# An HGRN2 stage inside a projection loop: small column-tiled products in two groups per unit instead of six, and a common PSUM bank for three levels

## The reference

```python
def hybrid_layer(x, ...):
    z = rmsnorm(x, norm_g) @ w_in          # 1024 -> 4608 columns
    ...
    q = jax.nn.silu(qc) * (C_KDIM ** -0.5)
    g = lbh + (1.0 - lbh) * jax.nn.sigmoid(fc)
    v = ic
    oc, s_fin = hgrn2(q, 1.0 - g, v, jnp.log(g), s0)

def hgrn2(q, k, v, logf, s0):              # scan over chunks
    def step(state, inp):
        bcum = jnp.cumsum(ft, axis=2)
        o_inter = einsum('bhld,bhdv->bhlv', qt * exp(bcum), state)
        diff = bcum[:, :, :, None, :] - bcum[:, :, None, :, :]
        decay = exp(where(causal, diff, -inf))
        attn = einsum('bhtd,bhtsd,bhsd->bhts', qt, decay, kt)
        o = o_inter + einsum('bhts,bhsv->bhtv', attn, vt)
        new_state = exp(blast) * state + einsum('bhsd,bhsv->bhdv', kt * exp(blast - bcum), vt)
        return new_state, o
```

## Time and profile before

| | us |
|---|---|
| median of 3 runs (lowest, highest) | 1688.76 (1685.87, 1689.35) |
| span of the profiled execution | 1690.4 |
| TensorE matmuls busy in it | 1588.9 (94%) |
| VectorE, ScalarE, GpSimd busy | 976.2 (58%), 823.9 (49%), 628.9 (37%) |
| HGRN stage, from the first to the last unit's steps | about 458 to 1075 |
| barrier between `front` and `attend_project` | about 1077 to 1080.7 |

### The profile page before, as it was taken

One profiled execution on the slowest core, in us unless ns is written; L12 is line 12 of the kernel. 1 busy time (PEld: TensorE's weight loads), 2 busy tenths in 40 slices (PEclk: granted clock), 3 DMA queues, 4 the chain that ended last, 5 costly groups with the idle time before them and its releaser, 6 DMA issues. The chain is left out here.

```text
span 1690.4 us, 38531 instructions
## 1 busy us (share of the span) xinstructions
PE 1588.9 (94%) x15345; PEld 1345.8 (80%) x15345; DVE 976.2 (58%) x2066; ACT 823.9 (49%) x1603; POOL 628.9 (37%) x754
## 2 busy tenths in 40 slices
PE   6999998899999999999999998899999888999997
PEld 5988887889988888878888787886777667777775
DVE  3436763433377777677676776325666556555652
ACT  4426876212256555566767776244777631111110
POOL 1102221200076666666666665203645602121110
PEclk9999998999999999999999999897999989999999
DMA  6310111124412212121110211447993284775651
GB/s 212 114 51 29 34 39 59 50 73 135 141 38 62 57 36 79 41 75 30 56 46 26 67 31 43 118 112 178 239 237 85 78 258 127 247 229 189 208 171 47
DMA packets 196287, 175.27 MB, mean 104 GB/s; under 512 B 84915, under 2 KB 180686, under 8 KB 193806
## 3 DMA queue, kind: packets, MB, share of 16 engines
q1 hardware_dynamic: 196110, 172.82, 35.6%
HBM read 123.18 MB, written 52.84 MB: 104 GB/s over the span
## 5 line engine op out<-in xcount | busy, mean ns | idle before, releaser
L49 PE MATMUL f_bank<-c_ht,c_whi 128*128 128x384 f32 (+1 forms) x864 | 321.0, 372 | 5.7 <-DVE c_wlo L893 5.7
L51 PE MATMUL f_bank<-c_ht,c_wlo 128*128 128x384 f32 (+1 forms) x864 | 303.3, 351 | 0.0
L50 PE MATMUL f_bank<-c_ht,c_whi 128*128 128x384 f32 (+1 forms) x864 | 302.9, 351 | 0.0
L842 ACT ACTIVATE f_scr<-f_scr 128x384 f32<-128x384 f32 (+1 forms) x210 | 114.0, 544 | 206.3 <-POOL f_scr L617 206.2
L1056 DVE TENSOR_TENSOR f_scr<-f_scr 128x192 f32<-128x192 f32 (+1 forms) x210 | 105.4, 502 | 137.4 <-ACT f_scr L842 137.1
L49 PEld LDWEIGHTS f_bank<-c_ht,c_whi 128*128 128x128 f32 x864 | 162.7, 188 | 21.4 <-DVE c_wlo L893 6.5
L50 PEld LDWEIGHTS f_bank<-c_ht,c_whi 128*128 128x128 f32 x864 | 163.2, 189 | 9.7 <-issue 1.1
L51 PEld LDWEIGHTS f_bank<-c_ht,c_wlo 128*128 128x128 f32 x864 | 163.0, 189 | 9.4
L616 POOL TENSOR_TENSOR f_scr<-f_scr 128x192 f32<-128x192 f32 (+1 forms) x210 | 134.6, 641 | 40.7 <-PE f_tps L1240 37.8
L1047 DVE COPY_PREDICATED f_scr<-f_scr,f_tps 128x384 f32<-128x384 int32 (+1 forms) x210 | 130.6, 622 | 18.1 <-PE f_tps L1240 9.5
L49 PE MATMUL a_s<-a_whi,a_mhi 128*128 128x512 f32 (+1 forms) x306 | 125.8, 411 | 4.5 <-DVE a_y L2471 4.5
(11 more groups left out here) (401 smaller groups left out, 3816.2 us busy)
## 6 DMA issues: line engine op xcount, KB each, us to landing
f_wraw<-in_w_in SPq DMA_DIRECT2D x27, 512.0 KB, 4.0
zs<-f_stage SPq DMA_DIRECT2D x48, 192.0 KB, 2.4
a_k<-in_ck SPq DMA_DIRECT2D x48, 192.0 KB, 5.7
a_v<-in_cv SPq DMA_DIRECT2D x48, 192.0 KB
f_scr<-in_xp SPq DMA_DIRECT2D x16, 512.0 KB, 4.2
a_x<-in_xp SPq DMA_DIRECT2D x16, 512.0 KB, 5.6
out_y_prompt<-a_y SPq DMA_DIRECT2D x16, 512.0 KB, 2.9
zt<-f_stage SPq DMA_DIRECT2D x38, 192.0 KB, 1.8
```

The lines of the kernel that those rows point to most:

```text
L49: nc.tensor.matmul(out, w_hi, m_hi, start=start, stop=False)
L50: nc.tensor.matmul(out, w_hi, m_lo, start=False, stop=False)
L51: return nc.tensor.matmul(out, w_lo, m_hi, start=False, stop=stop)
L842: A(lev[i % 3][:, :n], lev[i % 3][:, :n], ACT.Exp).then_inc(S["expd"], 1)
```

## The change

`HPLAN` is written anew, and with it:
- TensorE's small products of a unit stand in two groups. In slot 3: `hk`, `ho` of the unit before, and `hpa`: the diagonal, level 1, and one product for levels 64, 32 and 16 together. In slot 0: `hu` and `hpb` (levels 8, 4, 2). VectorE takes them in two rows of three, `hta` and `htb`; the states are `hv`.
- Pair products have three PSUM banks (`tps[0:3]`, the third shared with the transposes `kp`). Levels 64, 32 and 16 are written into one bank and taken with one mask, `far_mask`, the sum of their three; so a unit has six takes instead of eight. `level_blocks` cuts all blocks to 32 keys; `outputs` works in blocks of 32 instead of 64.
- Level 1 no longer goes through `hm`: its decay is the forget gate of one position, 1 - key. `h1`: ScalarE writes 1 - key into `gone` (Identity), VectorE multiplies the query in (`stepped_query`), and the product takes the key itself as its other side.
- `hgrn_gates` ends with the second table load; the two Ln are a step of their own, `hl`, in slot 4. The key's Ln takes the unscaled key with the scale inside; GpSimd scales the key in `hc1`, slot 0. `sqo` (the squared output) lies in PSUM.
- `hgrn_gates` of a unit now waits for the second pair product of the unit before (`2 * BURST * (v - 1) + 2`). `query` waits also for `qd_ready` and for all `xlev` of the unit before. `hk`'s transposes wait for the takes of the unit before; the merged product waits for `kd_copied`. `load_v` is issued at `hpa`.

```diff
-HPLAN = {0: [("hp6", 2), ("hm0", 1), ("hm1", 1)],
-         1: [("ho", 2), ("hpd", 1), ("hp0", 1), ("hd", 1), ("hm2", 1)],
-         2: [("hf", 2), ("hm3", 1), ("hp1", 1), ("hx", 1), ("hp2", 1), ("hm4", 1), ("he", 1), ("hw", 2), ("hk", 1)],
-         3: [("hu", 1), ("hm5", 1), ("hp3", 1), ("hg", 2), ("hs", 0)],
-         4: [("hm6", 1), ("hp4", 1), ("hn", 0)],
-         5: [("hp5", 1), ("hq", 0), ("hy", 0)]}
+NM = NL - 1
+BURST = 3
+HPLAN = {0: [("hu", 2), ("hpb", 2), ("htb", 2), ("hv", 2), ("hm0", 1), ("hc1", 1)],
+         1: [("hm1", 1), ("h1", 1)],
+         2: [("hm2", 1), ("hd", 1), ("hx", 1)],
+         3: [("hk", 1), ("ho", 2), ("hpa", 1), ("hta", 1), ("hf", 2), ("hs", 0), ("hm3", 1), ("hw", 2)],
+         4: [("hm4", 1), ("hm5", 1), ("hl", 0), ("he", 1), ("hn", 0)],
+         5: [("hq", 0), ("hy", 0), ("hg", 2)]}
...
-    return [(c, c + hs, hs) for c in range(0, P, 2 * hs)]
+    return [(c + x, c + hs, hs) for x in range(0, hs, QUAD) for c in range(0, P, 2 * hs)]
...
-        lp, kp, up = tps[0:2], tps[2], tps[3]
-        gnorm = op[:, 0:AW]
+        lp, kp, up = tps[0:3], tps[2], tps[3]
+        gnorm, sqo = op[:, 0:AW], op[:, FW // 2:FW]
...
-    pairs_of_level = lambda i: (NL + 1) * (i // NL) + i % NL + 2
+    pairs_of_level = lambda i: 2 * BURST * (i // NM) + max(i % NM + 1, BURST)
...
-                elif kind == "hs":
+                elif kind == "hc1":
                     h, g, t0, n, nt, _ = unit(a)
-                    pool.wait_ge(S["f_out"], BASE + a + 1)
+                    pool.wait_ge(S["log_k"], BASE + a + 1)
                     G.tensor_scalar(key[:, :n], key[:, :n], lbl[:, 1, h:h + 1], None, ALU.mult).then_inc(S["gated"], 1)
...
-                    act.wait_ge(S["pairs"], BASE + (NL + 1) * (v - 1) + 1)
+                    act.wait_ge(S["pairs"], BASE + 2 * BURST * (v - 1) + 2)
                     act.wait_ge(S["kd_turned"], BASE + v)
...
                 nc.scalar.preload_act_table_set(LOG_EXP)
+
+            def hgrn_logs(v):
+                h, n, x = v // NFG, unit(v)[3], cum[v % 2]
                 act.wait_ge(S["f_sig"], BASE + v + 1)
-                A(x, x, ACT.Ln, bias=lbl[:, 3, h:h + 1], scale=lbl[:, 1, h:h + 1]).then_inc(S["log_g"], 1)
-                act.wait_ge(S["gated"], BASE + v + 1)
-                A(rel[v % 2][:, :n], key[:, :n], ACT.Ln, bias=tiny[:, 0:1]).then_inc(S["log_k"], 1)
+                A(x[:, :n], x[:, :n], ACT.Ln, bias=lbl[:, 3, h:h + 1], scale=lbl[:, 1, h:h + 1]).then_inc(S["log_g"], 1)
+                act.wait_ge(S["f_out"], BASE + v + 1)
+                A(rel[v % 2][:, :n], key[:, :n], ACT.Ln, bias=tiny[:, 0:1], scale=lbl[:, 1, h:h + 1]).then_inc(S["log_k"], 1)
...
+                elif kind == "h1":
+                    n = unit(a)[3]
+                    act.wait_ge(S["gated"], BASE + a + 1)
+                    if a:
+                        act.wait_ge(S["pairs"], BASE + 2 * BURST * (a - 1) + 2)
+                    A(gone[:, :n], key[:, :n], ACT.Identity, bias=con["one"][:, 0:1], scale=-1.0).then_inc(S["g_one"], 1)
...
+            def pairs(v, i, *products):
+                nt = unit(v)[4]
+                x = 2 * BURST * v + i
...
+                if x >= BURST:
+                    pe.wait_ge(S["taken"], BASE + x - BURST + 1)
+                if i == 2:
+                    pe.wait_ge(S["kd_copied"], BASE + v + 1)
                 for j in range(nt):
+                    for left, right, hs in products:
+                        for k0, q0, w in level_blocks(hs):
+                            out = lp[x % BURST][k0:k0 + QUAD, j * P + q0:j * P + q0 + w]
+                            mm = nc.tensor.matmul(out, left[:, j * P + k0:j * P + k0 + QUAD], right[:, j * P + q0:j * P + q0 + w],
+                                                  start=True, stop=True)
...
+                elif kind == "hpa":
                     pe.wait_ge(S["gated"], BASE + a + 1)
                     pe.wait_ge(S["c_out"], BASE + a + 1)
+                    pairs(a, 0, (key, fq, 1))
+                    pe.wait_ge(S["g_query"], BASE + a + 1)
+                    pairs(a, 1, (key, gone, 1))
+                    pe.wait_ge(S["xlev"], BASE + NM * a + BURST)
+                    pairs(a, 2, *((lev[l], lev[l], HALVES[l]) for l in range(BURST)))
+                elif kind == "hpb":
+                    for l in range(BURST, NM):
+                        pe.wait_ge(S["xlev"], BASE + NM * a + l + 1)
+                        pairs(a, l, (lev[l - BURST], lev[l - BURST], HALVES[l]))
```

More of the change, by code:

```diff
@@ L308, in front @@
         cut = area(hc0, FW)
-        mask = [area(hc0 + FW + l * P, P) for l in range(NL)]
-        attn = area(hc0 + FW + NL * P, FW)
-        hk0 = hc0 + 2 * FW + NL * P
+        far_mask, mask = area(hc0 + FW, P), {l: area(hc0 + FW + (l - 2) * P, P) for l in range(3, NL)}
+        attn = area(hc0 + FW + 5 * P, FW)
+        hk0 = hc0 + 2 * FW + 5 * P
         kdt = area(hk0, FW)
-        vv, sg, oc, sqo = (area(hk0 + FW + r * FW // 2, FW // 2) for r in range(4))
+        vv, sg, oc = (area(hk0 + FW + r * FW // 2, FW // 2) for r in range(3))
+        gone = area(hk0 + FW + 3 * FW // 2, FW)
         sts = sb("sts", [P, 4 * NN])
@@ L558, in _ @@
                             sp.dma_start(zf[(row + h) * P:(row + h + 1) * P, SEQ:T], fs[:, x * NS:(x + 1) * NS]).then_inc(S["fs_store"], 16)
-                elif kind == "hu" and a % NFG == NFG - 1:
+                elif kind == "hv" and a % NFG == NFG - 1:
                     h = a // NFG
@@ L1025, in query @@
                 if v:
-                    dve.wait_ge(S["pairs"], BASE + (NL + 1) * (v - 1) + 1)
+                    dve.wait_ge(S["pairs"], BASE + 2 * BURST * (v - 1) + 1)
+                    dve.wait_ge(S["qd_ready"], BASE + v)
+                    dve.wait_ge(S["xlev"], BASE + NM * v)
                 V.scalar_tensor_tensor(out=fq[:, :n], in0=bank[c_at(v) % 3][:, :n], scalar=float(P) ** -0.5,
@@ L1044, in take @@
                     dve.wait_ge(S["o_sum"], BASE + v)
-                m = mask[i - 1] if i else con["ident"][:]
+                m = (con["ident"][:], mask[NL - 1], far_mask, mask[3], mask[4], mask[5])[i]
                 hold(dve, S["held"])
@@ L1048, in take @@
                                   m.bitcast(I32).unsqueeze(1).to_broadcast([P, nt, P]),
-                                  lp[x % 2][:, :n].rearrange("p (j t) -> p j t", t=P)).then_inc(S["taken"], 1)
+                                  lp[x % BURST][:, :n].rearrange("p (j t) -> p j t", t=P)).then_inc(S["taken"], 1)
             def multiply(v, l):
-                n, i, hs = unit(v)[3], NL * v + l, HALVES[l]
+                n, i, hs = unit(v)[3], NM * v + l, HALVES[l]
                 dve.wait_ge(S["expd"], BASE + i + 1)
@@ L1056, in multiply, with stepped_query @@
                 V.tensor_tensor(e[:, :, hs:], e[:, :, hs:], q[:, :, hs:], ALU.mult).then_inc(S["xlev"], 1)
+            def stepped_query(v):
+                n = unit(v)[3]
+                dve.wait_ge(S["g_one"], BASE + v + 1)
+                dve.wait_ge(S["c_out"], BASE + v + 1)
+                g, q = blocks(gone, n, 1), blocks(fq, n, 1)
+                V.tensor_tensor(g[:, :, 1:], g[:, :, 1:], q[:, :, 1:], ALU.mult).then_inc(S["g_query"], 1)
             def decayed_query(v):
@@ L1154, in _ @@
                     multiply(a, int(kind[2]))
-                elif kind == "hpd":
-                    take(a, 0)
-                elif kind[:2] == "hp":
-                    take(a, 1 + int(kind[2]))
+                elif kind in ("hta", "htb"):
+                    for i in range(BURST):
+                        take(a, BURST * (kind == "htb") + i)
+                elif kind == "h1":
+                    stepped_query(a)
                 elif kind == "he":
                     decayed_query(a)
-                elif kind == "hu":
+                elif kind == "hv":
                     states(a)
@@ L1244, in outputs @@
                 h, g, t0, n, nt, first = unit(v)
-                pe.wait_ge(S["taken"], BASE + (NL + 1) * (v + 1))
+                pe.wait_ge(S["taken"], BASE + 2 * BURST * (v + 1))
                 pe.wait_ge(S["s_new"], BASE + states_through(v))
@@ L1324, in _ @@
                     if a:
-                        pe.wait_ge(S["kd_copied"], BASE + a)
+                        pe.wait_ge(S["taken"], BASE + 2 * BURST * a)
+                    else:
+                        pe.wait_ge(S["k_copied"], BASE + 3 * NKP)
                     for j in range(nt):
```

64 lines of the change are left out of this document (28 added, 36 removed).

## The result

The changed kernel takes 1711.72 us (median of 4 runs, 1709.55 to 1713.24), the kernel before 1688.17 beside it: 1.0138 times as long, 95% interval 1.0124 to 1.0152. Forecast were 1682 us, range 1663 to 1701. It is 23.6 us slower, on rival 3's side and above its 1702.

A forecast was written before the change was run, and what follows sets the result against it. TensorE bounds the kernel now; afterwards a ring through all engines would. Five heads gain 16.5 us, the stage's end loses 2, leaving about 15; half clocks cost 8, so 7 us off: 1682 us, range 1663 to 1701.

The forecast's parts named there:

- rival 3: HGRN stage: ring slower than today, GpSimd levels and multiply towards their means by the SBUF lock; 1702 to 1713 us; chance 0.30.
- TensorE's part: HGRN stage: six visits become two, 1.3 us less per unit, plus 0.6 us less idle: 1.9 us in all.
- the ring: HGRN stage: chain from `hk` through gates, exponentials, Ln, scan and GpSimd levels to the next `hk`; 18.1 us per 384-column unit.
- the merged product: First burst: one product for levels 64, 32 and 16; 0.4 to 0.74 us, taken as 0.55.
- I take 18.1, nearer to the lower rows: Period chosen between 17.7 and 19.6 us, since VectorE is idle or reads PSUM for over half the GpSimd time.
- the lower sum: Lower end of the ring for 384 columns, 17.7 us, with GpSimd's levels as taken while VectorE is still.
- the clock: TensorE's stops before first bursts halve its clock: 0.7 us a fall, two falls a head, 8 us in all; bounds 0 and 23.
- Its point of decision: The slower-ring case decides from a mean period of 18.7 us for 384 columns on.
- rival 1: HGRN stage: the ring binds with some half clocks, 7 us off, 1682 us; chance 0.45, shared with another rival.
- two bursts: Sign in TensorE's timeline: two groups of small products per unit, none alone.
- the gates at the landing of the second pairs: Sign on ScalarE: the table load of `hs` starts when the second pairs land, 1.75 us into the ring.
- the bank of the c product covered: Second projection's product: its bank is freed by `hq` at 11.5 us of the ring and reached at 12.1, so covered.

The follow-up runs named there:

- j_three_and_scale: Changed kernel with scan before decayed query, key's scaling earlier, output norm's power later, and VectorE's weight scaling moved away from level 64: 1641.01 us, 0.9726 of the kernel before.
- a to d: Changed kernel with scan before decayed query (1666.94 us), key's scaling a slot earlier (1675.02), output norm's power behind level 2's difference (1678.35), all three together (1643.62).
- i_scale_moved: Changed kernel with VectorE's scaling of the next head's weights moved away from GpSimd's level-64 difference: 1698.86 us, 1.0063 of the kernel before.
- k_busy_where_idle: Changed kernel with twelve thrown-away products ahead of the `hk` transposes, only in the first three groups of a head: 1700.76 us, 1.0079 of the kernel before.
- d_all_three: Changed kernel with three moves: scan before decayed query, key's scaling before `hy`, output norm's power behind level 2's difference: 1643.62 us, 0.9728 of the kernel before.
- g_all_three_burst_twice: d_all_three with the second burst's pair products (levels 8, 4, 2) issued twice: 1681.36 us, 0.9955 of the kernel before.
- e_second_burst_twice: Changed kernel with the second burst's pair products (levels 8, 4, 2) issued twice: 1728.54 us, 1.0232 of the kernel before.
- f_busy_wait: Changed kernel with twelve thrown-away products of 256 columns ahead of the `hk` transposes in each unit but the first: 1707.79 us, 1.0116 of the kernel before.

## Why the prediction was wrong

- **TensorE's part** nearly held. Where the ring doesn't bind (j_three_and_scale) a head takes 8.1 us less than before, 1.6 a unit for 1.9. Outputs take 0.70 us (0.74). The exception is the merged product: of the 96 pair records the 48 that fill 0.4 us at the forecast pitch leave it about 0.76 us, my upper bound, where I took 0.55.
- **The ring** is the right mechanism, shown by a to d. The step that failed is its size as the sum took it, "I take 18.1, nearer to the lower rows": it is 18.7 us undisturbed, 1.0 over the lower sum, and 19.4 to 21.3 us where the weight scaling, a stop in the burst or the half clock came on top, of which only the clock had a term. (The lower sum's own terms give 17.8, not 17.7; nothing hangs on it.) Half of the 1.0 us lies ahead of the scan: merged pairs 0.5 us later, and `hw` 0.8 later, since it waits for takes of them; a column copy of 0.17 us for 0.69 gave some of it back. The other half lies behind it, 7.2 us for 6.7: three levels take 3.0 us for 2.8, and the exponential of `hx` waits 0.3 us behind a weight split on ScalarE.
- **What stands beside the ring's GpSimd work** was reasoned from VectorE's HGRN work alone. I left out the weight scaling, 1.0 us on level 64 in groups 2 and 3. A mean of 632 ns hid it, since it is two of many instructions. The unit at 800.0, with nothing else in it, takes 19.6 us for 18.7; i_scale_moved prices it at up to 13 us in all.
- **The stops inside the burst** were no term at all. Four of 1.2 to 2.0 us from 455 to 1060 us, 7 us together, in a burst that lies on the ring. They are read from the timelines; no run takes them away, so 7 us is an upper end and not a measured price; the unit at 1025.7, with a stop of 1.2 us alone, is 0.6 us over an undisturbed one.
- **The clock** cost about 11 us (k_busy_where_idle) for 8. Falls came at waits of up to 2.9 us, longer than the 1.3 to 2.2 forecast, and two behind the unforeseen stops. A fall lengthens a burst by up to 1.9 us (4.4 for 2.5) and the two units with nothing else by 1.0, not 0.7.
- Added up, 0.6 us of ring in some 17 periods (10 us), 13, 7 and 3 us more of clock are 33 us for the 30 that the forecast missed (an estimate, and the terms overlap: i_scale_moved took falls away with the collision). They meet where the time went: groups 2 and 3 are 1.9 and 2.4 us over their forecast, group 1 0.9, group 4 0.8, group 5 1.2. The last has no ring: there the j_three_and_scale period, 20.5, says that TensorE's own gain was 1.4 and not 1.9; the other 0.5 us is open.
- **Rival 3** had the side, the size (1702, 1713 for a ring of 19.6) and the collision; its stated cause, all levels at their means, is not what the trace shows: undisturbed half levels take mostly 0.5 to 0.6 us, and no undisturbed ring of 19.6 us was found. That its 1713 lies 1 us from the measured 1711.7 is luck. Its point of decision was right: 18.7 us undisturbed, and what comes on top decides. A ring taken only 0.8 us under the old period (18.1 for 18.9) deserved the same chance for this side as for rival 1.
- Where it was not wrong: two bursts, the gates at the landing of the second pairs, the second part as long as before, and the bank of the c product covered (TensorE waits for it once, 0.4 us).

## What to carry over

Gathering an engine's small steps into a burst makes that burst a meeting point: whatever must be ready before it and whatever waits for it close a ring through all engines. Sum up the ring with each engine's in-order neighbours, including other work that only shares a port, and then take off it what has no need to be there: three reorderings of the same steps turned 1.4% slower into 2.7% faster. And an idle gap ahead of a burst can be paid twice, once as the gap and once as the burst at half clock: here that was so for seven of eleven gaps of 2.3 to 2.9 us.

## What was not expected of the hardware

TensorE stops in the midst of small products, with no semaphore between them; in the kernel after for 1.2 to 2.0 us. TensorE goes on 2.2 to 3.0 us after a packet of the instruction queue, which moves 16 KB. For the stop that ends at 701.43 it is the one of 699 to 700 us, kernel after:

```profile
q8 instruction: 1, 0.02, 5.8%
```

Counting stops of 0.8 us and more from 455 to 1060 us, the kernel after has 4, d_all_three 6, g_all_three_burst_twice 9 and e_second_burst_twice 24; the one in d_all_three at 915 us stands four projection products behind a burst, the others of d_all_three inside one. All 43 end 2.2 to 3.1 us after such a packet. Before there are none. Not every fetch is followed by a stop: the whole program has 130 of them after and 122 before.

The numbers of packets say what they carry. e_second_burst_twice has 2304 matmuls more than the kernel after and 18 packets more: one for every 128 matmuls, each with its weight load. The other kernels fit: 936 matmuls and 8 packets more from before to after, 348 and 2 in f_busy_wait. A first burst of three tiles has 147 matmuls (3 transposes, 48 of the outputs, 96 of the pairs) that start within 2.5 us, so it can use up a whole packet's worth in less time than the 2.2 to 3.1 us from a packet to the next matmul. That a dense run of short instructions uses them up faster than they come is what I infer: e_second_burst_twice adds 72 short matmuls to a unit of three tiles, and 20 stops; f_busy_wait adds 12 long ones, and no stop. No run changed the number of instructions at the same work, so that stays open.
